# Splitting setup and finish between two engines, and reordering the output projection, in a streaming encoder step

## The reference

```python
def _rms(x, g):
    xf = x.astype(jnp.float32)
    y = xf * lax.rsqrt(jnp.mean(xf * xf, axis=-1, keepdims=True) + EPS)
    return (y * g.astype(jnp.float32)).astype(x.dtype)
...
    z = _rms(x, w["norm1_g"]) @ w["w_in"]
...
    o = jnp.concatenate([oa.reshape(B, S, -1), ob.reshape(B, S, -1), oc.reshape(B, S, -1), om.reshape(B, S, -1)], axis=-1)
    x = x + o @ w["w_o"]
...
    y, new["conv"] = _conv_ffn(_rms(x, w["norm2_g"]), prev, w["f_win"], w["f_conv_w"], w["f_conv_b"], w["f_wout"])
    return x + y, new
```

## Time and profile before

| | us |
|---|---|
| median of three executions | 3183.57 (3183.4 to 3184.96) |
| profiled execution, its own time | 3183.15 |
| span of the profiled execution | 3181.2 |
| PE busy | 2900.1 (91%) |
| DVE busy | 1747.1 (55%) |
| ACT busy | 1204.0 (38%) |

### The profile page before, as it was taken

The page is one execution under the profiler, slowest core; times in us unless marked ns, Lnnn a source line. Parts: engine busy times, 40 slices in busy tenths (PEclk is TensorE's granted clock), DMA queues, the critical chain, the costliest instruction groups (busy, mean ns, idle before and its releaser), DMA issues. The chain is left out here.

```text
span 3181.2 us, 49151 instructions
## 1 busy us (share of the span) xinstructions
PE 2900.1 (91%) x19106; PEld 2742.6 (86%) x19106; DVE 1747.1 (55%) x2837; ACT 1204.0 (38%) x2563; POOL 126.0 (4%) x248
## 2 busy tenths in 40 slices
PE   6888879899999999999978878789899999999997
PEld 5686868589999999999967768667899999999997
DVE  3467764743655555555645496466436555545554
ACT  5556544652322222222246574456423222221223
POOL 0200012000000000000001000120000000000000
PEclk8996989899999999999989889898899999999999
DMA  4110001121111111111031100101311111111111
GB/s 180 54 41 29 22 27 40 50 103 40 47 47 40 47 46 40 46 53 43 17 140 48 46 15 19 44 25 51 119 34 47 47 40 47 47 45 46 40 52 57
DMA packets 182256, 160.90 MB, mean 51 GB/s; under 512 B 14504, under 2 KB 169912, under 8 KB 181560
## 3 DMA queue, kind: packets, MB, share of 16 engines
q1 hardware_dynamic: 182072, 158.46, 15.7%
HBM read 129.57 MB, written 29.06 MB: 50 GB/s over the span
## 5 line engine op out<-in xcount | busy, mean ns | idle before, releaser
L1888 PE MATMUL ps<-h_hi,w_hi 128*128 128x352 f32 x2496 | 546.8, 327 | 20.7 <-DVE w_lo L1997 11.2
L1888 PE MATMUL ps<-h_hi,w_lo 128*128 128x352 f32 x2496 | 541.5, 324 | 0.0
L1888 PE MATMUL ps<-h_lo,w_hi 128*128 128x352 f32 x2496 | 541.4, 325 | 0.0
L1888 PEld LDWEIGHTS ps<-h_hi,w_hi 128*128 128x128 f32 x2496 | 428.1, 191 | 25.5 <-DVE w_lo L1997 11.6
L1888 PEld LDWEIGHTS ps<-h_hi,w_lo 128*128 128x128 f32 x2496 | 431.8, 189 | 0.0
L1888 PEld LDWEIGHTS ps<-h_lo,w_hi 128*128 128x128 f32 x2496 | 427.7, 189 | 0.0
L2331 ACT ACTIVATE cv<-up,cols 128x1058 f32<-128x1058 f32 x88 | 112.1, 1274 | 718.8 <-issue 678.7
L783 PE MATMUL ps<-w_hi,h_hi 128*128 128x256 f32 (+1 forms) x1088 | 316.5, 291 | 21.8 <-DVE w_lo L1011 20.0
L784 PE MATMUL ps<-w_lo,h_hi 128*128 128x256 f32 (+1 forms) x1088 | 310.8, 286 | 0.0
L2440 DVE TENSOR_TENSOR x_t<-ps,x_t 128x1056 f32<-128x1056 f32 x176 | 220.9, 1255 | 160.9 <-PE ps L1888 160.1
L785 PE MATMUL ps<-w_hi,h_lo 128*128 128x256 f32 (+1 forms) x1088 | 308.7, 284 | 0.0
(11 more groups left out here) (234 smaller groups left out, 4287.5 us busy)
## 6 DMA issues: line engine op xcount, KB each, us to landing
stage<-in_f_win SPq DMA_DIRECT2D x88, 512.0 KB, 3.7
stage<-in_f_wout SPq DMA_DIRECT2D x44, 512.0 KB, 3.6
stage<-in_w_in SPq DMA_DIRECT2D x40, 256.0 KB, 3.8
x_spill<-x_t SPq DMA_DIRECT2D x2, 4224.0 KB, 13.2
x_t<-x_spill SPq DMA_DIRECT2D x2, 4224.0 KB
w_raw<-in_w_in SPq DMA_DIRECT2D x24, 256.0 KB, 4.1
stage<-in_w_o SPq DMA_DIRECT2D x12, 512.0 KB, 4.0
o_raw<-o_spill SPq DMA_DIRECT2D x8, 528.0 KB, 5.0
```

The source lines that it names most:

```text
L1888: last = pe.matmul(ps[:, s0 + b, 0:BAND], lh, rh_[:, b * BAND:(b + 1) * BAND], start=(first_k and n == 0), stop=(last_k and n == 2))
```

## The change

- setup: x comes in two halves of four tiles (2 MB each) with the sample rows between them. The groups run g = 0 for all k, then g = 2, then g = 1. ACT copies g = 0 and 2 and then does all eight squares; DVE copies g = 1 and adds the squares two chunks behind. PE waits for each part of x at its first use.
- w_o_block: for m = 0 and 1, DVE adds the product before it makes `w_lo` of chunk m + 3. The square and `add_sq` of the last chunk leave the block.
- ffn_block: ACT squares chunk 7 into `prod` after `high_x(1)`, DVE adds it to `sumsq` after `low_x(1)` and signals `squares_full`. `mean(0)` and `mean(1)` move behind PE's chunk 1, `mean(2)` behind chunk 3; the roots move behind `high_x(4)` and `high_x(5)`.
- finish: `yo` holds four tiles; ACT copies the first half of each tile, DVE the second.

```diff
@@ setup
-        groups = [(k, g) for k in range(KC) for g in range(3)]
+        groups = [(k, g) for g in (0, 2, 1) for k in range(KC)]
+        x_sem = (S.data_loaded0, S.data_loaded1, S.loads_done)
...
-                sp.dma_start(x_in[:, 0:PT_TILES, :], I["x_prompt"][0].rearrange("(t p) d -> p t d", p=P)).then_inc(S.data_loaded0, 16)
-                sp.dma_start(x_in[0:DEC, PT_TILES, :], I["x_sample"][0]).then_inc(S.data_loaded1, 16)
+                sp.dma_start(x_in[:, 0:4, :], xv[:, 0:4, :]).then_inc(x_sem[0], 16)
+                sp.dma_start(x_in[0:DEC, PT_TILES, :], I["x_sample"][0]).then_inc(x_sem[2], 16)
+                sp.dma_start(x_in[:, 4:8, :], xv[:, 4:8, :]).then_inc(x_sem[1], 16)
@@ setup, tensor
-                pe.wait_ge(S.data_loaded0, 16)
-                pe.wait_ge(S.data_loaded1, 16)
+                    if k == 0:
+                        pe.wait_ge(x_sem[g], 16)
@@ setup, vector
-                add_squares(dve, sq)
+                for k in range(KC):
+                    n = 2 * KC + k
+                    dve.wait_ge(S.tr_done, n + 1)
+                    dve.tensor_copy(x_t[:, k, 512:1024], ps[:, n % 4, :]).then_inc(S.tr_low, 1)
+                    if k >= 2:
+                        add_squares(dve, sq, k - 2)
+                add_squares(dve, sq, KC - 2)
+                add_squares(dve, sq, KC - 1)
@@ w_o_block, scalar
+                    if m == KC - 1:
+                        break
                     act.wait_ge(S.x_added, m + 1)
@@ w_o_block, vector
                 for m in range(KC):
-                    if m + 3 < KC:
+                    if 2 <= m and m + 3 < KC:
                         split_w(m + 3)
                     dve.wait_ge(S.down_done, m + 1)
...
                     dve.tensor_tensor(xm, ps[:, s0:s0 + 3, 0:BAND], xm, ALU.add).then_inc(S.x_added, 1)
+                    if m < 2:
+                        split_w(m + 3)
...
-                add_sq(KC - 1)
@@ ffn_block, tensor
-                mean(0)
-                mean(1)
                 for k in range(KC):
                     pe.wait_ge(S.norm_lo, k + 1)
                     if k == 2:
+                        pe.wait_ge(S.squares_full, 1)
+                        mean(0)
+                        mean(1)
+                    if k == 4:
                         pe.wait_ge(S.norm_root, 1)
                         mean(2)
@@ ffn_block, scalar
-                root(0)
-                root(1)
+                act.activation(prod[:, :], x_t[:, KC - 1, :], ACT.Square).then_inc(S.x_ready, 1)
                 for k in range(2, KC):
+                    if k in (5, 6):
+                        root(k - 5)
                     high_x(k)
@@ ffn_block, vector
                     low_x(k)
+                    if k == 1:
+                        dve.wait_ge(S.x_ready, 1)
+                        dve.tensor_tensor(sumsq[:, :], sumsq[:, :], prod[:, :], ALU.add).then_inc(S.squares_full, 1)
@@ finish
-        yo = w.take("yo", [P, 2, D])
+        yo = w.take("yo", [P, 4, D])
...
+            @block.vector
+            def _(dve):
+                for t in range(TILES):
+                    r = tile_rows(t)
+                    dve.wait_ge(S.tr_done, 2 * t + 2)
+                    if t >= 4:
+                        dve.wait_ge(y_sem[t % 4], 16 * (t // 4))
+                    dve.tensor_copy(yo[0:r, t % 4, 512:1024], ps[0:r, (2 * t + 1) % 4, :]).then_inc(S.tr_low, 1)
```

More of the change, by code:

```diff
@@ L224, in build_program @@
         x_sq = sem("x_sq")
+        squares_full = sem("squares_full")
         h_ready = sem("h_ready")
@@ L251, in setup @@
         sq = Region(R_W2, R_END).take("sq0", [P, 2, T])
-        groups = [(k, g) for k in range(KC) for g in range(3)]
+        groups = [(k, g) for g in (0, 2, 1) for k in range(KC)]
+        x_sem = (S.data_loaded0, S.data_loaded1, S.loads_done)
+        copied = (S.tr_copied, S.tr_low, S.tr_copied)
         with nc.Block() as block:
@@ L262, in _ @@
             def _(sp):
-                sp.dma_start(x_in[:, 0:PT_TILES, :], I["x_prompt"][0].rearrange("(t p) d -> p t d", p=P)).then_inc(S.data_loaded0, 16)
-                sp.dma_start(x_in[0:DEC, PT_TILES, :], I["x_sample"][0]).then_inc(S.data_loaded1, 16)
+                xv = I["x_prompt"][0].rearrange("(t p) d -> p t d", p=P)
+                sp.dma_start(x_in[:, 0:4, :], xv[:, 0:4, :]).then_inc(x_sem[0], 16)
+                sp.dma_start(x_in[0:DEC, PT_TILES, :], I["x_sample"][0]).then_inc(x_sem[2], 16)
+                sp.dma_start(x_in[:, 4:8, :], xv[:, 4:8, :]).then_inc(x_sem[1], 16)
                 sp.dma_start(rope[:, 0:PT_TILES, :], consts["rope"].rearrange("(t p) c -> p t c", p=P)).then_inc(S.small_loaded, 16)
@@ L271, in _ @@
                 pe.wait_ge(S.pool_step, 2)
-                pe.wait_ge(S.data_loaded0, 16)
-                pe.wait_ge(S.data_loaded1, 16)
                 for n, (k, g) in enumerate(groups):
+                    if k == 0:
+                        pe.wait_ge(x_sem[g], 16)
                     if n >= 4:
-                        pe.wait_ge(S.tr_copied, n - 3)
+                        q = n - 4
+                        if q < 2 * KC:
+                            pe.wait_ge(S.tr_copied, q + 1)
+                        else:
+                            pe.wait_ge(S.tr_low, q - 2 * KC + 1)
                     for t in (range(4 * g, 4 * g + 4) if g < 2 else [PT_TILES]):
@@ L285, in _ @@
                 for n, (k, g) in enumerate(groups):
[L286 to L293, removed]
+                    if g != 1:
+                        act.wait_ge(S.tr_done, n + 1)
+                        c = 512 if g < 2 else DEC
+                        act.copy(x_t[:, k, 512 * g:512 * g + c], ps[:, n % 4, 0:c]).then_inc(S.tr_copied, 1)
+                for k in range(KC):
+                    act.wait_ge(S.tr_low, k + 1)
+                    if k == 0:
+                        act.wait_ge(S.tr_copied, 2 * KC)
+                    if k >= 2:
+                        act.wait_ge(S.x_sq, k - 1)
+                    act.activation(sq[:, k % 2, :], x_t[:, k, :], ACT.Square).then_inc(S.sq_done, 1)
             @block.vector
@@ L2491, in finish @@
         w = Region(R_Q, R_END)
-        yo = w.take("yo", [P, 2, D])
+        yo = w.take("yo", [P, 4, D])
+        y_sem = (S.out0, S.out1, S.out2, S.out3)
         with nc.Block() as block:
@@ L2500, in _ @@
                         if n >= 4:
-                            pe.wait_ge(S.tr_copied, n - 3)
+                            pe.wait_ge((S.tr_copied, S.tr_low)[g], t - 1)
                         for i in range(4):
@@ L2509, in _ @@
                     r = tile_rows(t)
[L2510 to L2515, removed]
+                    act.wait_ge(S.tr_done, 2 * t + 1)
+                    if t >= 4:
+                        act.wait_ge(y_sem[t % 4], 16 * (t // 4))
+                    act.copy(yo[0:r, t % 4, 0:512], ps[0:r, (2 * t) % 4, :]).then_inc(S.tr_copied, 1)
+            @block.vector
[3 more added lines that the diff above has]
+                    dve.wait_ge(S.tr_done, 2 * t + 2)
+                    if t >= 4:
+                        dve.wait_ge(y_sem[t % 4], 16 * (t // 4))
+                    dve.tensor_copy(yo[0:r, t % 4, 512:1024], ps[0:r, (2 * t + 1) % 4, :]).then_inc(S.tr_low, 1)
             @block.sync
@@ L2520, in _ @@
                     r = tile_rows(t)
-                    sp.wait_ge(S.tr_copied, 2 * t + 2)
+                    sp.wait_ge(S.tr_copied, t + 1)
+                    sp.wait_ge(S.tr_low, t + 1)
                     dst = O["y_prompt"][0, t * P:(t + 1) * P, :] if t < PT_TILES else O["y_sample"][0]
-                    sp.dma_start(dst, yo[0:r, t % 2, :]).then_inc((S.out0, S.out1)[t % 2], 16)
-                sp.wait_ge(S.out0, 16 * 5)
-                sp.wait_ge(S.out1, 16 * 4)
+                    sp.dma_start(dst, yo[0:r, t % 4, :]).then_inc(y_sem[t % 4], 16)
+                for q in range(4):
+                    sp.wait_ge(y_sem[q], 16 * len(range(q, TILES, 4)))
     setup()
```

## The result

The changed kernel takes 3167.53 us (median of five executions, 3166.51 to 3172.44) against 3183.95 before (five, 3183.4 to 3185.77): ratio 0.995, 95% interval 0.9932 to 0.9967. It is faster by 0.4 to 0.5%, and both intervals lie clear of 1. The forecast was 3169.3, with a range of 3165.0 to 3174.5.

What follows compares the result with a forecast made beforehand. TensorE, busy nearly throughout, was taken as the bound, except in setup and finish (copies, squares, stores). From 3183.15, setup -4.0, projections -8.0, heads +2.6 and finish -4.4 give -13.8, so 3169.3 us; range 3165.0 to 3174.5.

Steps and rivals of the forecast that it cites:

- the sum: Setup: VectorE's copies and adds take 14.5 us from about 16.7, ending at 31.2 instead of 35.2.
- Rival 2: Setup: the halves of x land together, VectorE ends 2.1 us later than now; 3175.4 in all, chance 0.07.
- the straight line through a store and a load: Setup: load time at 3.0 us a MB, so the first half lands about 7.2 us after issue.
- Rival 1: Output projection: the clock falls anyway, giving back 3.4 us; 3172.7 in all, chance 0.12.
- (a): FFN head: one add leaves the block before, so everything behind the barrier comes 1.36 us earlier.
- (b): FFN head: the two means now stand in TensorE's full list, costing 1.3 us more at full clock.
- (c): FFN head: the low clock, 5.9 us from the first matmul, falls wholly in the projection, costing 1.35 us more.
- Slack behind the reciprocal: FFN head: root, reciprocal and split after the third mean end with 1.6 us left before the first product.
- Rival 3: FFN head: it loses 2 to 3 us a layer, by late roots or longer low clock; 3173 to 3175, chance 0.1.
- rival 4: Setup and finish: transposes stay at the low clock, gaining only 3.1 and 1.9 us; 3172.8, chance 0.02.
- Rivals 5 and 6: Projection: the add waits for something else, 3177.4, chance 0.05; head: TensorE stays at low clock, 3214, chance 0.02.
- the good end of setup: Setup: with the first copy at 16.0 and 0.55 us a copy, 5.4 us less.

Runs made afterwards that it cites:

- late_x_two_buffers: The changed kernel, but TensorE waits for all of x before setup and finish has two buffers instead of four; 3188.27 us in one execution.
- finish_only: The kernel before with the new finish alone; 3182.98 us, ratio 0.9996.
- setup_only: The kernel before with the new setup alone; 3180.15 us, ratio 0.999.
- the two kernels with filler: The changed kernel, and the same with the old FFN head, each with eight unused matmuls a layer added; 3168.32 us and 3170.6 us.
- square_only: The kernel before with only the last square and the means moved into the FFN's head; 3186.51 us, ratio 1.0007.

## Why the prediction was right

**Setup, forecast -4.0.** Measured -4.07. The early half does it, as the sum has it, with the order of groups that lets TensorE use it; VectorE as a second engine, which the sum builds on, has no part in it. Rival 2 (halves landing together, 2.1 us later than now) was run in effect as late_x_two_buffers: 1.6 later. Two sizes were off. The first half landed 8.6 us after its issue at 0.75, not 7.2: the straight line through a store and a load was 1.4 too low, which cost little, since VectorE's first copy waits for the second half too (17.04, 16.7 forecast). A copy took 0.68 us and not 0.62, and yet VectorE's list took 14.1 us and not 14.5, because a copy and an add follow each other every 1.77 us, less than their sum of 1.93. That these nearly cancel is luck.

**Output projection, forecast -4.0 a layer.** Measured -3.8 in every projection beside before's own. It is gap (2.3) and low clock (1.5, forecast 1.7). The second part isn't always there to gain: in finish_only and setup_only one of the two unchanged projections took 73.86 us, 1.56 less than 75.42, with the gap still in it. Rival 1 was not seen in any of the sixteen changed projections, whose clock stayed at 1.00 throughout.

**Head, forecast +1.3 a layer.** The right sign, too large a size: +0.5 over ten heads a side. Terms (a) and (b), the earlier barrier and the means in the list, nearly cancel as forecast: -0.2 together by the two kernels with filler (30.04 against 30.23), -0.06 forecast. The term that was mis-sized is (c), the low clock: it was taken to last 5.9 us from TensorE's first matmul, and so to cost 1.35 more. It does not run from the first matmul. In each of the twenty heads without filler the clock fell 3.0 to 4.9 us after the start of the last add, while TensorE was idle, and stayed low for 6.8 us, whether TensorE's first work came 4.95 us (the means) or 6.26 us (the chunk) after that add. So with the moved square it was low for 3.6 to 5.4 us of the projection, and the +0.5 that was measured leaves 0.7 for (c). In layer 0 of the changed kernel the 3.6 happened to be the least, and that head shows no cost at all; the 5.4 of square_only's layer 0 is the most. What places the fall within these 2 us was not found. Slack behind the reciprocal was forecast at 1.6 and is 1.51. Rival 3 (2 to 3 us a layer) is out: the longest head took 32.50.

**Finish, forecast -4.4.** Measured 20.11 to 15.70; over the six profiles with the new finish as it stands 15.5 to 16.6, 16.0 in the mean, over the four with the old one 20.1 to 21.0, 20.4 in the mean. Stores bind, at 1.28 us for 512 KB (what the 410 GB/s of the window make), less than the 1.5 of the slope. That no tile would wait for a buffer was wrong: two did, for 0.6 and 0.7 us, at no cost that shows, since the DMA engines were full. TensorE's clock came up among transposes alone, as in the earlier trace rows, in the changed kernel too (0.50 with 6 in the window at 3152, 1.00 with 11 at 3157): rival 4 is out. But it came up 3.3 us after the first transpose, not 5.9. Rivals 5 and 6 have no trace either: the add moved up at once, and no head ran at the low clock throughout.

Two readings of the prediction are off without effect: by its own terms the good end of setup is 5.3 less, not 5.4, and the window at 733 puts the start of the low stretch at 733.30, not 733.35.

**The sum** of the local terms as measured is -4.1 - 7.6 + 1.1 - 4.4 = -15.0, against -13.8 forecast, -16.4 and -11.7 in the two measured medians. The difference of those two is within what the untouched stretches do by themselves. In the first profile of the changed kernel these are 5.2 us longer, 3.8 shorter and 1.3 shorter than before's, and come to nothing: that the total lies within 2 us of the forecast owes something to luck. "0.2% can be told" does for the whole change and not for a part: single runs of before go from 3176.1 to 3192.5 over 35 executions. A part of 4 us was only just told from none by its time (intervals up to 0.9998 and 0.9999), and its size is seen in a cut of the profile alone.

## What to carry to other kernels

Where an engine waits at the start for one large load, cut the load and order the work by what lands first, before giving the work to a second engine: here the cut with its new order was worth all of 4 us and the engine none. Where stores hold up copies, add buffers first: four instead of two were worth most of finish's 4.4 us. Put the instruction that frees a PSUM bank ahead of one that only feeds a later chunk; the list order of the evicting engine cost TensorE 2.3 us and, mostly, 1.5 more by its clock. To judge edits of a few us in a span of thousands, cut each profile at fixed instructions and compare lengths; the total also carries what the clock did elsewhere.

## What the hardware did that was not expected

The same instructions, on the same data, took 692.4 to 699.1 us between setup and the first projection in four profiles, and the windows show the reason in part: TensorE's clock at 0.50 at 216 us in one and 1.00 in another, with equal work. In the stretch from the first product of layer 0 to the cast of layer 1 the length goes along with the time at the low clock: 147 to 150 us of it in the three shortest (1449.8 to 1456.1), 171 in the four that took 1459.7 to 1459.9, 188 in the longest (1463.1). Up to the first projection it explains less: late_x_two_buffers, the longest there with 703.5, has the most low time, 175 us against 138 to 159, but among the others the two do not go together. What decides where the low stretches fall from one execution to the next was not tried. Eight matmuls without use a layer, some 5 us of TensorE, held the clock over the barrier (1.26 us idle) and shortened the head by 2.1 us.
